# A one-core decoder layer in float32: a new order inside the slots of the attention stage, and a new order and other PSUM banks for the last expert

## The reference, cut to what matters

```python
SEQ, D_MODEL, N_ATTN_HEADS, DV, DK = 1024, 1024, 4, 128, 64
N_GROUPS, EXPERTS_PER_GROUP, TOP_K, D_FF_EXPERT = 4, 8, 2, 512

def diff_attention(q, k, v, lam, lambda_init, subln_gain):
    for i in range(seq // Q_BLOCK):                      # 128 rows at a time, causal
        s = jnp.einsum('bqhmd,bkhmd->bhmqk', qb, kb) * scale      # two maps per head
        p = jax.nn.softmax(jnp.where(mask, s, -jnp.inf), axis=-1)
        a = p[:, :, 0] - lam * p[:, :, 1]
        outs.append(jnp.einsum('bhqk,bkhd->bqhd', a, vb))
    return rms_norm(jnp.concatenate(outs, axis=1), subln_gain) * (1.0 - lambda_init)

def reference(...):
    hn = rms_norm(x, attn_norm_gain)
    q, k, v, cb, cc, cu = jnp.split(hn @ w_in, splits, axis=-1)
    ...
    x = x + jnp.concatenate([attn_o, conv_o], axis=-1) @ w_out     # h
    hn2 = rms_norm(x, ffn_norm_gain)
    return x + hier_moe(hn2, w_group_router, w_expert_router, w_gate, w_up, w_down)

# hier_moe: per token the best of 4 groups, in it the best 2 of 8 experts, each expert is
#   (silu(xb @ w_gate[e]) * (xb @ w_up[e])) @ w_down[e]
# weighted by softmax(top 2) * (probability of the group)
```

## Time and profile before

| what | value |
|---|---|
| median of 3 runs | 1164.49 us (1161.64 to 1164.96) |
| the profiled execution | 1164.27 us, of which the span from the first to the last instruction is 1162.5 us |
| PE, share of the span | 94% |
| PEld / DVE / ACT / POOL | 74% / 73% / 59% / 31% |
| HBM read and written | 240.03 MB and 20.97 MB |
| mean granted clock of TensorE | 0.989 |

### The profile page before, as it was taken

The page is one execution under the profiler, slowest core; times in us unless marked ns, Lnnn a source line. Parts: engine busy times, 40 slices in busy tenths (PEclk is TensorE's granted clock), DMA queues, the critical chain, the costliest instruction groups (busy, mean ns, idle before and its releaser), DMA issues.

```text
span 1162.5 us, 15417 instructions
## 1 busy us (share of the span) xinstructions
PE 1094.4 (94%) x5621; PEld 858.4 (74%) x5621; DVE 851.3 (73%) x1208; ACT 680.4 (59%) x1003; POOL 355.5 (31%) x433
## 2 busy tenths in 40 slices
PE   5999999999879999889789999999999999999995
PEld 4999999889658777768567777777777777666663
DVE  6645354454676776667868998988988988888893
ACT  6424232222465655543567787787877877777783
POOL 2323333233421111121204424434344343222220
PEclk9999999999999999999899999999999999999999
DMA  8012030302301122323699999999999999999972
GB/s 244 2 54 55 19 92 1 91 19 91 128 6 45 66 92 91 127 92 121 252 392 375 370 377 373 372 375 374 369 376 379 361 370 362 367 356 367 373 308 46
DMA packets 77403, 253.64 MB, mean 218 GB/s; under 512 B 18832, under 2 KB 43408, under 8 KB 52752
## 3 DMA queue, kind: packets, MB, share of 16 engines
q1 hardware_dynamic: 70160, 235.85, 54.4%
q0 software_dynamic: 7168, 16.79, 6.2%
HBM read 240.03 MB, written 20.97 MB: 225 GB/s over the span
## 4 chain that ended last, share of the span: by engine, by line
PE 40%; DMA 10%; DVE 3%; ACT 1%; issue 1%; POOL 1%; POOLq 0%; SPq 0%; ACTq 0%; DVEq 0%
DMA raw<-in_w_gate 9%; PE banks L2115 8%; PE banks L2117 8%; PE banks L2116 8%; PE banks L2132 4%; PE banks L2134 4%; PE banks L2136 4%; PE banks L2091 1%; DVE wlo L2036 1%; PE banks L2100 1%; ACT whi L1985 1%; DMA xn_rows<-hn 0%; DMA out<-y_sb,table_i 0%; PE banks L1656 0%; PE banks L1658 0%
## 5 line engine op out<-in xcount | busy, mean ns | idle before, releaser
L2036 DVE TENSOR_TENSOR wlo<-raw,whi 128x2048 fp32r<-128x2048 f32 x190 | 427.9, 2287 | 52.2 <-ACT whi L1985 52.1
L1985 ACT CAST whi<-raw 128x2048 fp32r<-128x2048 f32 x188 | 354.0, 1910 | 39.9 <-DMA raw<-in_w_gate 24.1
L2115 PE MATMUL banks<-whi,rT_hi 128*96 128x512 f32 x512 | 206.6, 403 | 7.2 <-DVE wlo L2036 6.3
L1967 POOL DMA_INDIRECT out<-y_sb,table_i x32 | 149.2, 4663 | 202.4 <-ACT y_sb L2003 197.2
L2117 PE MATMUL banks<-whi,rT_lo 128*96 128x512 f32 x512 | 202.6, 396 | 0.0
L2116 PE MATMUL banks<-wlo,rT_hi 128*96 128x512 f32 x512 | 201.5, 394 | 0.0
L2115 PEld LDWEIGHTS banks<-whi,rT_hi 128*96 128x96 f32 x512 | 82.8, 162 | 42.9 <-DVE wlo L2036 7.3
L2117 PEld LDWEIGHTS banks<-whi,rT_lo 128*96 128x96 f32 x512 | 82.8, 162 | 36.3 <-issue 0.5
L2116 PEld LDWEIGHTS banks<-wlo,rT_hi 128*96 128x96 f32 x512 | 83.3, 163 | 31.2 <-issue 0.3
L1958 POOL DMA_INDIRECT rows<-xn_rows,table_i x30 | 50.0, 1666 | 182.3 <-PE banks L2091 182.3
L871 ACT ACTIVATE qk_sq<-banks 128x256 f32<-128x256 f32 x32 | 12.3, 385 | 129.8 <-PE banks L1514 129.8
(11 more groups left out here) (250 smaller groups left out, 2037.3 us busy)
## 6 DMA issues: line engine op xcount, KB each, us to landing
raw<-in_w_gate SPq DMA_DIRECT2D x64, 1024.0 KB, 23.8
raw<-in_w_up SPq DMA_DIRECT2D x64, 1024.0 KB, 24.1
raw<-in_w_down SPq DMA_DIRECT2D x64, 1024.0 KB, 27.4
c_raw<-in_w_in SPq DMA_DIRECT2D x12, 512.0 KB, 3.7
q_raw<-in_w_in SPq DMA_DIRECT2D x12, 512.0 KB, 6.2
x_stage<-in_x SPq DMA_DIRECT2D x8, 512.0 KB, 6.6
wo_raw<-in_w_out SPq DMA_DIRECT2D x2, 2048.0 KB, 7.7
h_sb<-in_x SPq DMA_DIRECT2D x8, 512.0 KB, 5.2
```

The costliest lines, as they stand in the source:

```text
L1967: pool.indirect_dma_start(out=s.out_rows, out_offset=bass.IndirectOffsetOnAxis(ap=s.table_i[:, e:e + 1], axis=0), in_=s.y_sb[e % 2][:], in ...
L1985: act.copy(s.w_hi[i % HI][:], s.raw[i % RING][:]).then_inc(s.hi_ready, 1)
L2036: dve.tensor_tensor(s.w_lo[i % RING][:], s.raw[i % RING][:], s.w_hi[i % HI][:].bitcast(F32), ALU.subtract).then_inc(s.lo_ready, 1)
L2115: pe.matmul(o, s.rT_hi[e % 2][:, c, :], hi[:, c4, :], start=(c == 0), stop=False)
```

## The change

It has two parts. In the slots: `turn_h` of part 0 moves from the end of the h0 slot to just ahead of its fill, part 1 from inside the h1 slot to the end of the h0 slot; `copy_hnT` follows (part 0 after the h0 slot's exponents, part 1 at the start of the h1 slot). The gate exponents move from h0 to h1, `weigh_tokens` from h1 to h2 (there ahead of `choose_group`), and DVE does `low_oT` right after `mix`, ahead of `route_piece`. In the last expert: DVE does `hidden(31)` ahead of the split of tile 190 and `low_hid(31)` ahead of the split of tile 191; `down(31, ...)` writes banks 0 and 1, which expert 30's gate and up products used, and waits for `hid_ready` of expert 30 instead of its y.

```diff
@@ scalar, slots @@
                 if turn_b_at(g) is not None:
-                    copy_hnT(turn_b_at(g), 0)
+                    copy_hnT(turn_b_at(g), 1)
                 if g >= 2:
                     square_o(g - 2)
                 if g >= 1:
                     copy_maps(g - 1, 0)
-                if turn_b_at(g) is not None:
-                    copy_hnT(turn_b_at(g), 1)
                 exponent(g, 0)
                 if g >= 1 and tile_head(g - 1)[0] >= 4:
                     copy_maps(g - 1, 1)
                 exponent(g, 1)
+                if turn_a_at(g) is not None:
+                    copy_hnT(turn_a_at(g), 0)
                 if g >= 2:
                     round_oT(g - 2)
-                if g % HEADS == 0 and weights_at(g) is not None:
+                if g % HEADS == 1 and weights_at(g) is not None:
@@ vector, route_piece @@
+                if r == 2 and 0 <= j - 1 < FIRST:
+                    weigh_tokens(j - 1)
                 if r == 2 and 0 <= j < FIRST:
                     choose_group(j)
...
-                if r == 1 and 0 <= j - 1 < FIRST:
-                    weigh_tokens(j - 1)
@@ vector, slots @@
                 mix(g)
-                route_piece(g)
                 if g >= 2:
                     low_oT(g - 2)
+                route_piece(g)
@@ tensor, slots @@
                 score(g, 0)
-                if turn_b_at(g) is not None:
-                    turn_h(turn_b_at(g), 1)
...
+                if turn_a_at(g) is not None:
+                    turn_h(turn_a_at(g), 0)
                 i, q = fill_at(g)
...
                 if turn_a_at(g) is not None:
-                    turn_h(turn_a_at(g), 0)
+                    turn_h(turn_a_at(g), 1)
@@ experts @@
+    def down_bank(e):
+
+        return gate_banks(E - 2) if e == E - 1 else 2
...
+        hidden(E - 1)
         split_lo(tile_of(E, 4))
-        hidden(E - 1)
+        low_hid(E - 1)
         split_lo(tile_of(E, 5))
-        low_hid(E - 1)
         dve.wait_ge(s.used, PLACE[E - 1, 5] + 1)
         dve.wait_ge(scattered, (E - 2) * 16)
+        dve.wait_ge(y_ready, E - 1)
...
                 pe.wait_ge(hT_lo_ready, e + 1)
-                if e >= 1:
+                if e == E - 1:
+                    pe.wait_ge(hid_ready, e)
+                elif e >= 1:
                     pe.wait_ge(y_ready, e)
```

More of the change, by code:

```diff
@@ L2027, in scalar @@
         act.wait_ge(scattered, (E - 2) * 16)
-        act.copy(s.y_sb[(E - 1) % 2][:, 0:512], ps[0:SLOTS, 2, :]).then_inc(y_ready, 1)
+        act.copy(s.y_sb[(E - 1) % 2][:, 0:512], ps[0:SLOTS, down_bank(E - 1), :]).then_inc(y_ready, 1)
     def vector(dve):
@@ L2131, in down @@
                 for n in range(2):
[L2132 removed]
+                    pe.matmul(ps[0:SLOTS, down_bank(e) + n, :], s.hidT_hi[e % 2][:, c, :], hi[:, c2, n * 512:(n + 1) * 512], start=(c == 0), stop=False)
                 for n in range(2):
[L2134 removed]
+                    pe.matmul(ps[0:SLOTS, down_bank(e) + n, :], s.hidT_hi[e % 2][:, c, :], lo[:, c2, n * 512:(n + 1) * 512], start=False, stop=False)
                 for n in range(2):
[L2136 removed]
+                    ins = pe.matmul(ps[0:SLOTS, down_bank(e) + n, :], s.hidT_lo[e % 2][:, c, :], hi[:, c2, n * 512:(n + 1) * 512], start=False, stop=(c == FC - 1))
             ins.then_inc(s.used, 1)
```

5 lines of the change are left out of this document (1 added, 4 removed).

## The result

The changed kernel takes 1156.34 us (median of 4 executions, 1153.77 to 1157.54) against 1163.95 us for the kernel before beside it: a ratio of 0.9931, 95% interval 0.9915 to 0.9946, so about 8 us faster. Repeated later, beside another set of runs of the kernel before, it was 0.9929 (0.9912 to 0.9947). The forecast was 1158.5 us, with a range of 1153.5 to 1162.6.

A forecast was written before the change was run, and what follows sets the result against it. PE was taken to bound the slots, with short holes, and the weight stream the experts, passing saved time on. From 1164.27 us, 3.0 for the slots and 2.8 for the end gave 1158.5 us, range 1153.5 to 1162.6.

The forecast's parts named there:

- (a): Slots: PE's waits for the copies of turned h go, 5.0 us in 7 waits.
- (b): Slots: `route_tile`'s waits for `low_oT` go, 3.0 us in 6 waits.
- (g): h1 slots: the gain is not whole, since PE then meets `low_oT` itself; 6.4 of 8.0 us left.
- (d): Narrow h0 slots: part 0 of `turn_h` fills the fill's wait for `mc_lo`, 0.9 us gained in 2 waits.
- (h): Slots: nothing taken from `turn_maps`' "issue" waits, since DVE is late there and `add_x` and `mc_lo` come as late.
- (e): h2 slots: `weigh_tokens`, free in h1, delays `add_x` and the next `low_qt`; costs 4 x 0.63 = 2.5 us.
- (f): h2, h3 and h0 slots: DVE idles for ma_hi before the early `low_oT`; 1.8 us lost at PE, an estimate.
- (c): Narrow slots: `turn_maps` waits for `low_oT`, shown as "issue", 2.6 us in 5 waits; counted only in the upper bound.
- The exponents: Slots: gate exponents no longer stall ACT in h0 for `choose_second`; that stall hid behind PE and DVE, costed at nothing.
- Rival 3: Slots: early `low_oT` makes DVE wait for ACT in every h2, h3 and h0 slot; slower, 1167.5 us; chance 0.07.
- The clock: Late slots: one half-clock stretch costs 1.7 us, which shorter waits could win; a rival, not a term.
- rival 1: Slots: all waits go, DVE's delays find cover and the half-clock stretch goes; 1150.9 us, with half 1154; chance 0.17.

The follow-up runs named there:

- last_banks: Kernel before with only the last expert's product moved to banks 0 and 1, DVE's order and slots as before: 1163.25 us, ratio 0.9991.
- slots_only: Kernel before with only the slots part of the change, last expert as before: 1159.05 us, ratio 0.9958.
- turns_only: Kernel before with only the turned rows of h and their copies moved: 1163.25 us, ratio 0.9983.
- turns_exp: Kernel before with turned rows and copies moved, exponents and `weigh_tokens` a slot later, no early `low_oT`, last expert as before: 1158.63 us, ratio 0.9960.
- best: Changed kernel with `weigh_tokens` back in h1 and `low_oT` behind the routing in h3 slots only: 1151.51 us, ratio 0.9897; repeated 1152.16 us, 0.9903.
- weigh_h1: Changed kernel with `weigh_tokens` put back into h1 behind `normalise_h`, exponents in h1: 1155.17 us, ratio 0.9919 to the kernel before.
- low_first: Kernel before with only `low_oT` moved ahead of the routing piece: 1167.74 us, ratio 1.0027.
- turns_low: Kernel before with turned rows of h, their copies and `low_oT` moved; exponents, `weigh_tokens` and last expert as before: 1162.59 us, ratio 0.9988.
- last_only: Kernel before with only the last expert's part of the change, slots as before: 1161.01 us, ratio 0.9978.

## Why the prediction was right

**The regime and the passing on.** In 13 of the 14 traces, this case's kernels and variants, the first steady load starts anywhere from 563.8 to 575.8 us, while the time from it to the last rounding is 565.0 to 567.7 (569.3 in the last, that of `last_banks`). What the stream is given at its start it hands on, within 2.7 us of its own scatter. From the start of the last slot to that first load are 40.5 to 41.4 us, but for the 43.5 of `slots_only`. "If the steady stream starts as before" and "the last tile does not" can both be put away.

**Slots: 3.0 us forecast, 4.9 measured** (3.0 to 6.8 by the interval of the slots part alone). The terms, with the lengths of the table:

- (a), (b), (g), the h1 slots: 6.4 forecast. Taking the length without a half-clock stretch where another trace in the old order has it (10.19 for tile 4, 9.58 for tile 0), the six h1 slots lost 10.9 us, of which six turns of 0.45 have only moved to h0 (2.7): 8.2 won. The waits behaved much as forecast: in these six slots PE's waits were 8.0 us and are 2.1 in the changed kernel, so 5.9 of them went (of the rest 0.9 is L1686; the others are new and small, 0.3 to 0.5 each, for the maps in tile 4 and in `turn_o` in tiles 1 and 0). The other 2.3 us stand in no row of waits. Tile 6's h1 slot shows where they come from, before and after:

```profile
374.03 0.38 PE L1560 MATMUL banks<-ident,q_dup 128*128 128x128 f32 x2
374.86 1.95 PE L1686 MATMUL banks<-w_route,hnT 128*128 128x36 f32 x16 [0.45 <-DVE ma_lo L1205]
```

```profile
371.20 0.38 PE L1560 MATMUL banks<-ident,q_dup 128*128 128x128 f32 x2
371.42 1.87 PE L1686 MATMUL banks<-w_route,hnT 128*128 128x36 f32 x16
```

  From the first of these rows to the second are 0.83 us with a wait of 0.45, and 0.22 without it: 0.61 won by a wait that counts 0.45. PE's rows overlap (the two turns of q begin 0.11 apart and are 0.27 long), so a wait's row holds only what is left beyond the end of the row before it, and a short wait shows in no row at all. In the same slot the fill begins 0.47 behind the first of the last three turned maps before (369.06 to 369.53) and 0.25 after (366.44 to 366.69), with no wait listed in either. The prediction priced each wait at its row; this is the term that was mis-sized most.
- (d), `turn_h` in the place of the mc_lo wait: 0.9 forecast. The h0 slots of tiles 1 and 0, where that wait was, grew by 0.45, of which 0.9 are moved turns: 0.45 won, half of the forecast, since `turn_h` itself now waits there for `add_x`, 0.74 and 0.96 us:

```profile
482.03 0.66 PE L1672 MATMUL banks<-ident,h_sb 128*128 128x128 f32 x4 [0.74 <-DVE h_sb L1215]
```

  This is no new lateness. (h) had said that `add_x` comes as late as the wait of `turn_maps` now ends; (d) left out that `turn_h` needs `add_x` too. It takes the early read as well: `turns_only` and `turns_exp`, with the turned rows in the same place, and `best`, with the late read in h3, have no wait of `turn_h` on h_sb.
- (e), `weigh_tokens` in h2: -2.5 forecast, 4 x 0.63; `weigh_h1` gives 28.08 - 25.56 = 2.5. The term is exact for the h3 slots. What was wrong is the sentence "in h1 it was free": once PE's other waits were gone it stood in front of the read that `route_tile` waits for, as `turns_only` shows (5.7 us of waits) and `turns_exp` (2.4).
- (f), `low_oT` before the routing: -1.8 forecast. The h3 slots of tiles 5, 2 and 1 grew by 2.4, of which `weigh_h1` takes 1.9 back; the rest is 0.5, or 0.6 with as much for tile 4 (an estimate, since its old h3 slot follows a half-clock stretch). The h0 slots of tiles 4 and 2 grew by 0.7 more than the moved turns, and `best` gives these 0.7 back: 1.3.
- (c), (h): the "issue" waits fell from 2.6 to 0.4, but nothing was won by it, as (h) had it, since DVE is the late engine there. In the h0 slots of tiles 1 and 0 they came back as the waits on h_sb, in the h3 slots of tiles 2 and 1 as waits of `turn_o` for `scale_o` (0.90 and 1.39 us). The longer waits for the maps are others: in the h3 slots of tiles 5 and 4 they went from 0.33 and 0.53 to 1.12 and 1.43, and in the h0 slot of tile 2 from 1.22 to 1.78.

8.2 + 0.45 - 2.5 - 1.3 = 4.9. That this meets the 4.9 of the ratio to the tenth is chance, with an interval of 3.0 to 6.8, and it leaves the half-clock stretches out. Against the forecast the h1 slots gave 1.8 more and (f) cost 0.5 less, and (d) gave 0.5 less. The prices also hold only in this company: against `turns_exp` the early read costs 2.5 us in the h3 and h0 slots and wins 2.7 in the h1 slots, next to nothing, and the ratios of the two kernels (0.9960 and 0.9958) say the same.

**The exponents: costed at nothing**, and no run has their move alone, so its own price isn't shown. But the reason was wrong. "ACT's stall hid behind PE and DVE" was true of the kernel before, with 4.4 us of it; with the early read it is 8.5 us and PE waits for what stands behind it (`low_first`, 1.0027). In the changed kernel ACT has no wait of L976 in the slots at all. Without the move the early read loses alone and wins nothing beside the turned rows (`turns_low` 0.9988 against 0.9983 of `turns_only`), so a cost of nothing in the sum hid a condition of another term. Rival 3, slower, came true for that edit alone. Its own mechanism, DVE's wait for ma_hi, is there too (13.1 us in `low_first`, 2.8 before). By the slots both share the loss: the six h1 slots are as long as before (59.5 us), since ACT's stall took back there what the waits of L1686 gave; the h3 slots of tiles 5, 2 and 1 are 0.5 longer and the h0 slots of tiles 4, 2 and 1 0.9 (8.26, 8.14 and 6.99 us), where DVE is late.

**The clock** was a rival for 1.7 us (rival 1's condition, with half of 3.4 us as the price of a stretch). Four traces in the old order of the slots have 3, 4, 2 and 4 half-clock stretches there and a length from first to last slot of 231.1, 230.6, 228.2 and 231.2 us; three in the new order have 1, 2 and 1 and lengths of 223.9, 224.3 and 223.9. The profiled execution of before has three, that of after one. The stretches aren't strewn at random. All four old ones have one at 442.5 to 443.8, and tile 4's h2 slot is then 7.8 to 7.9 us long, as in `turns_only` (444.37), against 6.6 in the nine other traces; how much of it comes back in the next slot isn't shown, since every kernel without the stretch has another order there. All four also have one between 324 and 331, as has one of the three new ones, and all three new ones have one at 519.8 to 520.9. So in these traces the new order lost the stretch at 443 and kept one near 522, the one that the prediction's rival looked at. A stretch costs between nothing (at 330 us in `last_only`, among the waits of tile 7's first two slots: 14.46 us for both, against 14.54 in `slots_only` without it) and 1.6 us (tile 1's h2 slot, 6.27 against 4.71). So of the 7.2 us between the profiled executions, some 2 are the clock. The Trainium skill ("TensorE: Matmul & The Clock Gate", section "Why this matters for your kernels") says that idle gaps between bursts of matmuls throw the engine back. It means gaps longer than any of these waits, so the traces neither confirm nor refute it, and the prediction's "by that rule" stretched it. What they show is this: `turns_only` has four stretches behind waits of 0.8 to 0.9 us, the kernel before has a wait of 0.84 at the same place (L1686 at 409.26) with none, and the changed kernel has waits of 1.78 and 1.44 us (L1604 at 456.28 and 448.57) with no stretch near, though `weigh_h1` has one right behind the first of them. So a single wait doesn't decide, and what does is open.

**The end: 2.8 us forecast, 2.35 measured** in the trace and 2.6 in the ratio of `last_only`. The order of events was right, and so was what is late next: expert 30's scatter, 5.48 us against 5.40. What was mis-sized is the step after it. The forecast let the last scatter start 0.1 us after that landing. It landed at 1142.88 and POOL's DMA starts at 1143.64, 0.76 later, where one that waits for a copy of y starts 0.3 after the copy (1153.97 to 1154.25 before).

**The named signs**: waits on hnT under 0.5 (none), L1686 at about 1.2 (0.9), waits on mapsT in the wide h3 slots longer by 0.6 (0.8 and 0.9), the start of the stream at 571.6 (566.6), last rounding at 1137.5 (1132.25), from there 10.9 us (11.39). The start differs by more than the slots' gain since the first slot began 1.5 us earlier; over all traces it begins between 301.3 and 303.2, in a stage that the change doesn't touch. Together the difference of the two spans is 1.5 (before the slots) + 7.15 (slots) - 0.6 (last slot to first load) + 0.25 (stream) + 2.35 (end) - 0.1 (after the scatter) = 10.5 us.

## What to carry to other kernels

A move that is priced at nothing because a wait is covered has to be priced again under each of the other moves: here the turned rows alone won 2 us (within an interval that holds nothing as well) and the early read alone lost 3, while all the slot moves together won 4.9, and two of them were remedies for the same wait, of which one sufficed. Where an engine's rows overlap, as PE's do here, read a row of waits as the least that its removal wins: 5.9 us of rows gave 8.2 us. When a wait is removed from the bounding engine, look for the small work that was "free" just behind it in the stream of its supplier; putting each such piece where its supplier idles was worth another 3 to 4 us (by the slots 2.5 + 0.7). And in a tail, ask first for the transfer that the last one has to wait for: bringing its input forward (1.9 us) was worth several times a bank of its own (0.3 to 0.7).

## What the runs showed of the hardware

The half-clock stretches last 3.4 us or a multiple, but for the one in which the program ends, and their place varies in part between executions of one order. In the slots between 340 and 545 us the 14 traces have 24 of them, and 18 begin 0.2 to 3.3 us behind the first row of a `route_tile`, 16 matmuls of 36 columns in a h1 slot. The waits around these are of every size: 0.8 to 0.9 us in `turns_only`, 0.5 in the changed kernel (519.75), 0.3 in `best` (493.17). But the traces hold 84 such `route_tile`s, so this is a place where they gather and no rule. In the old tail PE waits 1.77 us for `turn_hid`; of the seven traces that have this wait, three have a half-clock stretch right behind it (at 1138.92 in `turns_low`, 1145.17 in `low_first`, 1146.95 in `last_banks`), and of the seven others, where it is gone, none (before the last scatter). Two of them, by window:

```profile
1138.92:1142.34 3.42, 3.42 (x10) 1.95 (x8) 1.28 (x2) 0.00 (x0) 0.00 (x0) 0.50 0.00 0
```

```profile
1145.17:1148.59 3.42, 3.42 (x9) 2.22 (x8) 1.48 (x2) 0.02 (x1) 0.00 (x0) 0.50 0.00 0
```

The last scatter comes 15.5 and 15.3 us behind the last rounding there, against 13.7 to 13.9 in the four with the old order of the tail and no stretch. So part of what the last expert's order wins (0.9969, or 3.6 us, where its distance gives 1.9) may be these stretches; three of seven at 1.6 us would be 0.7 on average (an estimate), and the rest is within the interval.
